# Stick-breaking attention by running products of sigmoids instead of sums of logarithms

## The reference, cut to what matters

```python
def stick_breaking_attention(q, k, v):
    """q,k,v (B,H,S,Dh). A[t,s] = sig(z_ts) prod_{s<j<t} (1 - sig(z_tj)), s < t strictly."""
    ...
        z = jnp.einsum("bhqd,bhkd->bhqk", q_blk, k_blk).astype(jnp.float32) * scale
        mask = k_pos[None, :] < q_pos[:, None]
        log_not = jnp.where(mask, jax.nn.log_sigmoid(-z), 0.0)
        suffix = lax.cumsum(log_not, axis=3, reverse=True) - log_not
        log_w = jax.nn.log_sigmoid(z) + suffix
        att = jnp.where(mask, jnp.exp(log_w), 0.0)
        outs.append(jnp.einsum("bhqk,bhkd->bhqd", att.astype(v.dtype), v_blk))
```

## Time and profile before

| what | value |
|---|---|
| median of 3 runs | 2297.96 us (2297.16 to 2303.62) |
| the profiled execution's own time | 2292.51 us |
| its span from first to last instruction | 2290.7 us |
| PE busy in the span | 2126.0 us (93%) |
| DVE, ACT, POOL busy | 1101.4, 813.8, 103.5 us |
| mean granted TensorE clock | 0.957 of full |
| changed stage, first score matmul to last copy | 237.3 to 339.7 us of the span |

### The profile page before, as it was taken

How to read it: one execution, slowest core, us unless ns; L and a number is a source line. 1 busy time by engine, 2 the same in 40 slices (tenths; PEclk the granted TensorE clock), 3 DMA queues, 4 the chain that set the end, 5 groups by cost and what they waited for, 6 DMA issues and landing times. The chain is left out here.

```text
span 2290.7 us, 30020 instructions
## 1 busy us (share of the span) xinstructions
PE 2126.0 (93%) x12032; PEld 1686.6 (74%) x12032; DVE 1101.4 (48%) x1737; ACT 813.8 (36%) x1271; POOL 103.5 (5%) x134
## 2 busy tenths in 40 slices
PE   6999785997999899799999999999999899999997
PEld 5888551784888787688888877886566578888886
DVE  4553227445544353447777334313666655432433
ACT  3112653223323242334444213223455544422331
POOL 0000000660000000000000001000000000000000
PEclk9999796997999999899999998988999999999998
DMA  4323000000332233022323233320111122233322
GB/s 148 101 92 103 21 1 0 3 3 1 94 102 93 99 113 120 19 83 101 99 93 106 100 137 118 99 74 19 37 39 38 38 83 87 97 98 96 100 93 83
DMA packets 47853, 173.54 MB, mean 76 GB/s; under 512 B 5144, under 2 KB 7448, under 8 KB 47488
## 3 DMA queue, kind: packets, MB, share of 16 engines
q1 hardware_dynamic: 45440, 162.99, 21.7%
q0 software_dynamic: 1728, 8.23, 1.1%
q10 hardware_dynamic: 576, 0.84, 0.1%
HBM read 169.90 MB, written 2.13 MB: 75 GB/s over the span
## 5 line engine op out<-in xcount | busy, mean ns | idle before, releaser
L198 DVE TENSOR_TENSOR weights_lo<-weights_raw,weights_hi 128x1024 fp32r<-128x1024 f32 (+2 forms) x288 | 363.6, 1263 | 802.9 <-ACT weights_hi L190 802.7
L190 ACT ACTIVATE weights_hi<-weights_raw 128x1024 fp32r<-128x1024 f32 (+2 forms) x288 | 313.5, 1088 | 875.1 <-PE end_ps L223 245.6
L221 PE MATMUL sp_ps<-arena_parts,weights_hi 128*128 128x512 f32 x720 | 283.6, 394 | 10.8 <-DVE arena_parts L282 10.3
L223 PE MATMUL sp_ps<-arena_parts,weights_lo 128*128 128x512 f32 x720 | 281.6, 391 | 0.0
L222 PE MATMUL sp_ps<-arena_parts,weights_hi 128*128 128x512 f32 x720 | 281.6, 391 | 0.0
L221 PE MATMUL end_ps<-arena_parts,weights_hi 128*128 128x512 f32 x576 | 224.8, 390 | 2.2 <-DVE arena_parts L2723 1.7
L223 PE MATMUL end_ps<-arena_parts,weights_lo 128*128 128x512 f32 x576 | 224.1, 389 | 0.0
L222 PE MATMUL end_ps<-arena_parts,weights_hi 128*128 128x512 f32 x576 | 224.1, 389 | 0.0
L221 PEld LDWEIGHTS sp_ps<-arena_parts,weights_hi 128*128 128x128 f32 x720 | 136.3, 189 | 41.1 <-issue 12.0
L222 PEld LDWEIGHTS sp_ps<-arena_parts,weights_hi 128*128 128x128 f32 x720 | 136.3, 189 | 28.7 <-issue 0.7
L223 PEld LDWEIGHTS sp_ps<-arena_parts,weights_lo 128*128 128x128 f32 x720 | 136.0, 189 | 28.6
(11 more groups left out here) (392 smaller groups left out, 3514.5 us busy)
## 6 DMA issues: line engine op xcount, KB each, us to landing
weights_raw<-w_up SPq DMA_DIRECT2D x44, 512.0 KB, 3.4
weights_raw<-w_proj SPq DMA_DIRECT2D x38, 512.0 KB, 3.4
weights_raw<-w_gates SPq DMA_DIRECT2D x32, 576.0 KB, 3.7
weights_raw<-w_ca SPq DMA_DIRECT2D x32, 512.0 KB, 3.4
weights_raw<-w_down SPq DMA_DIRECT2D x16, 704.0 KB, 4.1
weights_raw<-w_in SPq DMA_DIRECT2D x22, 512.0 KB, 3.4
weights_raw<-w_logits SPq DMA_DIRECT2D x16, 512.0 KB, 3.5
weights_raw<-w_ff1a SPq DMA_DIRECT2D x16, 512.0 KB, 3.4
```

Source lines behind the costliest of these rows:

```text
L190: act.activation(self.w_hi[:, g % 2, 0:cols], self.raw[:, g % 2, 0:cols], ACT.Copy).then_inc(self.hi_ready, 1)
L198: dve.tensor_tensor(self.w_lo[:, g % 2, 0:cols], self.raw[:, g % 2, 0:cols], self.w_hi[:, g % 2, 0:cols].bitcast(F32), ALU.subtract).then_ ...
L221: pe.matmul(out, left[0], right[0], start=start, stop=False)
L223: return pe.matmul(out, left[1], right[0], start=False, stop=stop)
```

## The change

Only `stick_breaking_stage` changes. The scores are made with queries on the partitions and keys along the row, for two heads (a "pair", `c`, sides 0 and 1) at a time: their matmuls alternate between rows 0 to 63 and rows 64 to 127 of PE. A head's three "parts" `m` are the three banks: query block 3 against 512 keys, block 2 against 384, and blocks 1 and 0 together (256 and 128 keys).

ACT takes two Sigmoids of each part: of -z into `keep` and of z into `stop`. POOL masks the diagonal block of `keep` with a strictly lower triangle (`below`). DVE runs a `tensor_tensor_scan` from the right end of each row to the left (state = keep x state + begin, with `begin` the identity in the diagonal block), which leaves the running product in place. The weight is `stop` times the product one column to the right: DVE for parts 0 and 1, POOL (`last_part`) for part 2. PE transposes the weights block by block into the bank that held the scores (`turn`), ACT copies them to SBUF (`place`), and PE makes the output for both heads with interleaved column halves. Each part is handed on by itself; `scores(c + 1, m)` waits until both transposed parts m of pair c are placed. POOL also fills `begin` and clears the `att` buffers at the start of the stage (the `made` semaphore); before, it had no work in this stage.

The diff, without the removed lines, which stand above, and without declarations of semaphores:

```diff
...
+    flat = lambda tile: core.arena[:, tile:tile + 5, :].rearrange("p a t -> p (a t)")
+    pair_of = lambda tile: [flat(tile)[:, b * 1280:(b + 1) * 1280] for b in range(2)]
+    keep, stop, att = pair_of(38), pair_of(43), pair_of(63)
+    begin = [core.arena[:, 48, :], core.arena[:, 48, P:], core.arena[:, 49, 0:384]]
+    below = core.arena[:, 50, 0:P]
+    att_t = [core.arena[:, 55 + 4 * b:59 + 4 * b, :].rearrange("p j (i t) -> p j i t", t=P) for b in range(2)]
+    PARTS = [(0, 512), (512, 384), (896, 384)]
+    BLOCKS = [(3, 0, 0), (2, 1, 0), (1, 2, 0), (0, 2, 256)]
...
+    order = [(c, m, side, 6 * c + 2 * m + side) for c in range(NW) for m in range(3) for side in range(2)]
...
+        bank = lambda h, m: ps[:, 3 * (h % 2) + m, :]
+        part = lambda buf, h, m: buf[h % 2][:, PARTS[m][0]:PARTS[m][0] + PARTS[m][1]]
...
             @block.tensor
             def _(pe):
...
+                def scores(c, m):
+                    if c >= NW:
+                        return
+                    if c:
+                        pe.wait_ge(placed, 6 * (c - 1) + 2 * m + 2)
+                    for i, _, lo in (x for x in BLOCKS if x[1] == m):
+                        for side in range(2):
+                            rows = slice(HD * side, HD * side + HD)
+                            mm = pe.matmul(bank(side, m)[:, lo:lo + (i + 1) * P], query[rows, c, i * P:(i + 1) * P], key[rows, c, 0:(i + 1) * P],
+                                           start=True, stop=True)
                     mm.then_inc(scores_ready, 1)
...
+                def turn(c, m, side):
+                    h = 2 * c + side
+                    if m < 2:
+                        pe.wait_ge(att_ready, 4 * c + 2 * m + side + 1)
+                    else:
+                        pe.wait_ge(last_ready, h + 1)
+                    for i, _, lo in (x for x in BLOCKS if x[1] == m):
+                        for j in range(i + 1):
+                            cols = slice(lo + j * P, lo + (j + 1) * P)
+                            mm = pe.transpose(bank(h, m)[:, cols], part(att, h, m)[:, cols], core.c("ident"))
+                    mm.then_inc(turned, 1)
+                def output(c):
+                    pe.wait_ge(placed, 6 * c + 6)
                     if c >= 2:
                         pe.wait_ge(out_taken, c - 1)
                     for j in range(NT):
...
+                        for side in range(2):
+                            h = 2 * c + side
+                            mm = pe.matmul(ps_out[HD * side:HD * side + HD, c % 2, j * P:T], value[:, j, h * HD:(h + 1) * HD],
+                                           att_t[side][:, j, j:NT, :].rearrange("p i t -> p (i t)"), start=(j == 0), stop=(j == NT - 1),
+                                           skip_group_check=True)
                     mm.then_inc(out_done, 1)
...
+                for m in range(3):
+                    scores(0, m)
+                pe.wait_ge(made, 4)
+                for c in range(NW):
+                    for m in range(3):
+                        for side in range(2):
+                            turn(c, m, side)
+                        scores(c + 1, m)
+                    output(c)
+            @block.gpsimd
+            def _(pool):
+                pool.memset(begin[0], 0.0).then_inc(made, 1)
+                pool.memset(begin[2], 0.0).then_inc(made, 1)
+                pool.wait_ge(made, 2)
+                pool.tensor_copy(begin[0][:, T - P:], core.c("ident"))
+                pool.tensor_copy(begin[2][:, P:384].rearrange("p (n t) -> p n t", t=P),
+                                 core.c("ident").unsqueeze(1).broadcast_to([P, 2, P])).then_inc(made, 1)
+                pool.memset(flat(63), 0.0).then_inc(made, 1)
+                pool.wait_ge(below_ready, 1)
+                def last_part(c):
+                    for side in range(2):
+                        pool.wait_ge(left, 6 * c + 5 + side)
+                        for lo, hi in ((0, 256), (256, 384)):
+                            ins = pool.tensor_tensor(part(att, side, 2)[:, lo:hi - 1], part(stop, side, 2)[:, lo:hi - 1],
+                                                     part(keep, side, 2)[:, lo + 1:hi], ALU.mult)
+                        ins.then_inc(last_ready, 1)
+                for c, m, side, at in order:
+                    h, n = 2 * c + side, PARTS[m][1]
+                    blocks = 1 if m < 2 else 2
+                    pool.wait_ge(keep_ready, at + 1)
+                    diag = part(keep, h, m)[:, n - blocks * P:].rearrange("p (n t) -> p n t", t=P)
+                    pool.tensor_tensor(diag, diag, below.unsqueeze(1).broadcast_to([P, blocks, P]), ALU.mult).then_inc(masked, 1)
+                    if c and m == 0 and side == 1:
+                        last_part(c - 1)
+                last_part(NW - 1)
             @block.scalar
             def _(act):
...
+                def breaks(c, m, side, at):
+                    h, n = 2 * c + side, PARTS[m][1]
+                    act.wait_ge(scores_ready, 3 * c + m + 1)
+                    act.activation(part(keep, h, m), bank(h, m)[:, 0:n], ACT.Sigmoid, scale=-1.0).then_inc(keep_ready, 1)
+                    act.activation(part(stop, h, m), bank(h, m)[:, 0:n], ACT.Sigmoid).then_inc(stop_ready, 1)
+                def place(c, m, side, at):
+                    if c < 0:
+                        return
+                    act.wait_ge(turned, at + 1)
+                    own = [x for x in BLOCKS if x[1] == m]
+                    for i, _, lo in own:
+                        ins = act.activation(att_t[side][:, 0:i + 1, i, :], bank(side, m)[:, lo:lo + (i + 1) * P].rearrange("p (j t) -> p j t", t=P),
+                                             ACT.Copy)
+                    ins.then_inc(placed, 1)
+                for c in range(NW + 1):
+                    for m in range(3):
+                        for side in range(2):
+                            place(c - 1, m, side, 6 * (c - 1) + 2 * m + side)
+                        if c < NW:
+                            for side in range(2):
+                                breaks(c, m, side, 6 * c + 2 * m + side)
             @block.vector
             def _(dve):
...
+                def weights(c, m, side, at):
+                    h, n = 2 * c + side, PARTS[m][1]
+                    run = part(keep, h, m)
+                    dve.wait_ge(masked, at + 1)
+                    dve.wait_ge(stop_ready, at + 1)
+                    dve.tensor_tensor_scan(run[:, ::-1], run[:, ::-1], begin[m][:, ::-1], 0.0, ALU.mult, ALU.add).then_inc(left, 1)
+                def multiply(c, m, side, at):
+                    h, n = 2 * c + side, PARTS[m][1]
+                    dve.wait_ge(left, at + 1)
+                    dve.tensor_tensor(part(att, h, m)[:, 0:n - 1], part(stop, h, m)[:, 0:n - 1], part(keep, h, m)[:, 1:n], ALU.mult)\
+                       .then_inc(att_ready, 1)
                 def take(c):
...
+                    dve.wait_ge(out_done, c + 1)
                     dve.tensor_copy(core.arena[:, 4 + c, :], ps_out[:, c % 2, :]).then_inc(out_taken, 1)
...
+                dve.scalar_tensor_tensor(below, core.c("neg_tri"), -1.0, core.c("ident"), ALU.mult, ALU.subtract).then_inc(below_ready, 1)
+                dve.wait_ge(made, 4)
+                for c in range(NW):
+                    for m in range(3):
+                        for side in range(2):
+                            weights(c, m, side, 6 * c + 2 * m + side)
+                        for side in range(2):
+                            if m < 2:
+                                multiply(c, m, side, 6 * c + 2 * m + side)
+                        if c and m == 1:
+                            take(c - 1)
                 take(NW - 1)
```

More of the change, by code:

```diff
@@ L529, in stick_breaking_stage @@
     value = core.arena[:, 34:38, :]
[L530 to L534, removed]
-    scores_ready = core.sem("sb_scores_ready")
[L536 to L541, removed]
+    flat = lambda tile: core.arena[:, tile:tile + 5, :].rearrange("p a t -> p (a t)")
[6 more added lines that the diff above has]
+    BLOCKS = [(3, 0, 0), (2, 1, 0), (1, 2, 0), (0, 2, 256)]
+    made = core.sem("sb_made")
+    below_ready = core.sem("sb_below_ready")
+    scores_ready = core.sem("sb_scores_ready")
+    keep_ready = core.sem("sb_keep_ready")
+    stop_ready = core.sem("sb_stop_ready")
+    masked = core.sem("sb_masked")
+    left = core.sem("sb_left")
     att_ready = core.sem("sb_att_ready")
+    turned = core.sem("sb_turned")
+    placed, last_ready = core.sem("sb_placed"), core.sem("sb_last_ready")
+    order = [(c, m, side, 6 * c + 2 * m + side) for c in range(NW) for m in range(3) for side in range(2)]
     out_done = core.sem("sb_out_done")
@@ L561, in _ @@
             def _(pe):
[L562 to L568, removed]
-                    mm.then_inc(scores_ready, 1)
@@ L571, in weights @@
[L571 to L580, removed]
@@ L587, in output @@
                     for j in range(NT):
```

(4 more changed lines are left out.)

14 lines of the change are left out of this document (removed).

## The result

The changed kernel takes 2261.74 us (median of 4 runs, 2259.28 to 2264.57) against 2298.11 us: a ratio of 0.9845, 95% interval 0.9832 to 0.9859. Forecast were 2267.5 us and a range of 2250 to 2286. The profiled execution took 2259.28 us, its span 2257.5 us.

A forecast was written before the change was run, and what follows sets the result against it. It took a loop through ACT's table loads to bound the old 102.4 us stage. Start 4.4, four pairs 58.6, end 4.9 and clock 4 us gave 72 us, a gain of 30.4, so 2267.5 us, range 2250 to 2286.

The forecast's parts named there:

- What bounds the kernel before: Old stage, 102.4 us: bound by a loop through ACT, with 17 table loads of 21.8 us, not by PE.
- Start, 4.4 us: Start of the new stage: POOL's memsets and copies ahead of the first mask take 4.4 us.
- DVE and POOL, 14.7 us a pair: Each pair's period: DVE and POOL work one at a time, scans 5.8, products 2.5 and POOL 6.4 us.
- Each of these is shorter than the 14.7 us: Added waits between PE, ACT and POOL: each shorter than DVE's and POOL's 14.7 us, if PE is at full clock.
- The clock, 4 us: PE at half clock between bursts: 4 us over the stage, bounds none and 30 us.
- four equal turns of 14.65 us: The middle of the new stage: four pairs, together 58.6 us.
- End, 4.9 us: End of the new stage: last transposes 0.5, copies 0.7, output 3.0 and its copy 0.7 us.
- Next stage, no change taken: Table loads for Tanh and Sigmoid after this stage: 1.3 us either way, none counted.
- Half clock through the stage: Rival, 0.13: PE at half clock through the stage adds 4.9 us a pair; stage 88 us, 2283 us.
- Side by side does not overlap: Rival, 0.06: the two heads' matmuls do not overlap, scores 2.7 us more; stage 83 us, 2278 us.
- No full turns: Rival, 0.20: DVE and POOL do not alternate fully, ACT sets about 12 us a pair; stage 57 us, 2253 us.
- In series: Rival, 0.06: hand-offs run one after another, 32.7 us a pair, sign over 25; stage 140 us, 2336 us.

The follow-up runs named there:

- before_one_table: The kernel before the change with its Ln replaced by a second Exp, leaving one table load instead of 17; stage 101.8 us instead of 102.3.
- combined: Changed kernel without masks, all products on DVE, short clearing, output behind the next pair's part 1, copy one pair later; ratio 0.9785, stage 55.5 us.
- coarse: Changed kernel with a pair handed on whole between its copies and the next scores, last_part behind its own pair's masks; stage 73.6 us.
- mult_dve: Changed kernel with the products of part 2 on DVE behind its scans, so POOL has only masks; 2250.25 us, stage 60.0 us.
- filler: Changed kernel with unused identity matmuls on PE before each group of transposes and scores, 12 a pair; stage 61.1 us.
- in_order_fill: Changed kernel in its own order, without masks, all products on DVE, short clearing, plus unused identity matmuls on PE; ratio 0.9782, stage 53.8 us.
- serial_sides: Changed kernel with the two heads' score and output matmuls one side after the other instead of alternating; stage 73.6 us.
- no_mask: Changed kernel without POOL's masks, scans starting from 0 with the diagonal 1 from begin, part 2 scanned in two pieces; ratio 0.9803, stage 59.3 us.
- combined_fill: The kernel of combined with unused identity matmuls added on PE; ratio 0.978, stage 53.4 us.

## Why the prediction was right, and where not

The total was right: 2261.7 us against 2267.5, a gain of 36.4 us where 30.4 were forecast. Its parts were less so.

- **What bounds the kernel before: wrong.** I let the waits overrule PE's 89 us and named a loop through ACT with 21.8 us of table loads. `before_one_table` shows that the loads were not on the path: without 16 of them the stage kept all but 0.5 us. PE was the bound there: between two pairs, 291.15 to 312.26 us, its matmuls leave it idle for only 0.8 of 21.1 us, at full clock. DVE's 36.8 us behind ACT were the idle time of an engine with little to do. It did no harm to the sum, because I built the new stage from nothing. What the change takes off that bound is PE's work: the 14 weight matmuls of a head, 5.4 us at full clock.
- **Start, 4.4 us: right, a little dear.** The first mask starts 3.75 us into the stage and the first scan 4.3 (242.34), behind POOL's memsets.
- **DVE and POOL, 14.7 us a pair: mechanism right, size near, role wrong.** The scans run backwards and in place at 1.21 and 0.94 us without POOL beside them (1.15 and 0.88 forecast; `combined`). Beside POOL they take up to 1.64, and four POOL products 3.77 us, where alone they took 2.52 (`coarse`). That is nearly what full turns look like. The rule of the Trainium skill (SBUF — State Buffer, SBUF: two separate sides) is full turns, and the trace agrees in the main, not to the tenth: the mask at 269.50 ends 0.25 us after the scan that held it up, where alone it takes 0.46. At least one of the two is active for 13.0 us of a period, DVE's copy of 0.7 included, against 14.7 us of prices in turn. And I wrote that there would be hardly a moment in which neither works. There are 4.0 us of them in each period.
- **"Each of these is shorter than the 14.7 us": the step that failed.** The added waits close a loop of 16.96 us through all four engines. I named `last_part` behind the next masks and `scores` behind `placed`, and took each for itself instead of walking round once. `mult_dve` takes one position out of it: 9.4 us less, up to 4.1 of them through the clock. The distance between two outputs, forecast as 15 us, is 17.
- **The clock, 4 us: far too small.** I had bounded it by 0 and 30 and taken a value near the lower end, since PE had slack. The engine with slack stood in the loop, and the whole first pair ran at 0.50; `filler` gives back 8.3 us even though its own products stand in PE's queue.
- **How the errors met, which is luck.** Forecast were four equal turns of 14.65 us, an end of 4.9 and 4 us for the clock on top. Measured from first scan to first scan, the first turn takes 9.8 us, since no earlier pair's products and output stand in it: 4.8 less than forecast. The next two take 16.9 and 17.0: 4.5 more. The last with the end takes 21.5: 1.9 more. All of the clock is in these times already, so its 4 us go. That is 72 less 2.5, and no turn came within 1.9 us of its number. At full clock the sum was 67.9; `filler`, at 0.89, has 61.1.
- **End, 4.9 us: right.** From POOL's last product to the last copy it is 4.4 us, the output 2.38 us at full clock. PE's prices held as well: 0.11 us a transpose, and both heads' scores in 2.43 us at full clock (`in_order_fill`, start) where one head took 2.42; 2.7 were forecast.
- **Next stage, no change taken, bounds 1.3 either way.** Tanh and Sigmoid both run without a load, and PE's first matmul comes 1.22 us after the stage's first instruction instead of 2.65: 1.4 us gained. The Trainium skill (ScalarE: Activation LUTs, Table sets) has Tanh in the set of Sigmoid, and the trace agrees.

```profile
307.74 0.63 ACT L756 ACTIVATE arena<-arena 64x512 f32<-64x512 f32 x1 [3.47 <-PEq L559]
...
308.28 0.61 ACT L757 ACTIVATE arena<-arena 128x512 f32<-128x512 f32 x1
...
308.94 1.22 PE L773 MATMUL tm_ps<-arena 64*128 64x512 f32 x1 [2.24 <-ACT arena L757]
```

- **The rivals.** "Half clock through the stage" was half true: 0.67 in the mean. "Side by side does not overlap" is out: the output took 2.38 us for both heads at full clock, and `serial_sides` lost 4.2 us. "No full turns" missed with its 57 us, although the turns are not quite full. "In series" is out by its own sign, 25 us a pair, but it named the place: `scores` behind `placed` is in the loop.

What stays open: what sets the period once the masks are gone (`no_mask`), how much of the 9.4 us of `mult_dve` is place and how much clock, and how much of the 8.3 us of `filler` each group of matmuls carries; none was taken apart.

## What to carry to other kernels

When several engines hand tiles round, write the loop down once, from an instruction to its own successor a turn later, and add it up; engine sums alone are a lower bound, and an instruction's place in its queue can cost more than its work (`last_part`: 9.4 us for 2.5 of work, the clock's part included). Before an engine's share of work is called slack, ask at what clock it will run when it has slack. A total of idle time under "waits" names who waits, not what the bound is: take the suspected cost away and look.

## What the runs showed of the hardware that I had not expected

- Products of the identity that nobody reads raised PE's granted clock in the periods from 0.71 to 1.00 and made the stage 8.3 us shorter. With matmuls that are longer because they don't overlap (`serial_sides`) it was 0.82.
- A backward scan in place costs hardly more than the forward one of the earlier trace rows: 1.21 us for 128x512 (`combined`) against 1.15 to 1.19.
- The first scores of the stage took 4.64 us at a clock of 0.50 or 2.43 us at 1.00, with the same code up to there (`combined_fill`, `in_order_fill`).
- 17 table loads, 21.8 us of ACT time, were hidden to within 0.5 us.
